# First two branches of a three-branch block: merge products that follow single y tiles, values turned behind two gate tiles, wide value products

## The reference, cut to what matters

```python
(a_q, a_f, a_i, a_z, b_q, b_k, b_v, b_o, b_ig, b_fg, b_z,
 c_r, c_k, c_v, c_wd, c_ad, c_z, g_a, g_b, g_c) = split_cols(xn @ w_in[l])
# first branch: chunked linear attention over 8 heads of 128, values a_i
y_a = head_rmsnorm(o, norm_g) * jax.nn.silu(z.astype(f32))
# second branch: 4 heads, queries and keys 128 wide, values b_v 256 wide
num = scores @ v                  # the kernel takes the whole sequence as one chunk
h = num / jnp.maximum(jnp.abs(den), jnp.exp(-m_t))[..., None]
y_b = head_layernorm(h, norm_g, NORM_EPS) * jax.nn.sigmoid(o_raw) * jax.nn.silu(z)
merged = (jax.nn.sigmoid(g_a) * (y_a @ w_br[l, 0])
          + jax.nn.sigmoid(g_b) * (y_b @ w_br[l, 1])
          + jax.nn.sigmoid(g_c) * (y_c @ w_br[l, 2]))
h = h + merged @ w_out[l]
```

## Time and profile before

| | |
|---|---|
| median of 3 runs | 3596.31 us (3595.64 to 3598.92) |
| profiled execution | 3597.59 us, span 3595.8 us |
| TensorE busy | 3515.2 us, 98% |
| TensorE weight loads | 2942.6 us, 82% |
| VectorE busy | 1504.8 us, 42% |
| ScalarE busy | 486.2 us, 14% |
| mean granted TensorE clock | 0.994 |
| line 411 (merge products) | 169.9 us busy, 9.6 us idle before |
| line 380 (gate products) | 343.5 us busy, 0.7 us idle before |

### The profile page before, as it was taken

The page is one execution under the profiler, slowest core; times in us unless marked ns, Lnnn a source line. Parts: engine busy times, 40 slices in busy tenths (PEclk is TensorE's granted clock), DMA queues, the critical chain, the costliest instruction groups (busy, mean ns, idle before and its releaser), DMA issues.

```text
span 3595.8 us, 47831 instructions
## 1 busy us (share of the span) xinstructions
PE 3515.2 (98%) x20239; PEld 2942.6 (82%) x20239; DVE 1504.8 (42%) x2787; ACT 486.2 (14%) x1113; POOL 26.9 (1%) x58
## 2 busy tenths in 40 slices
PE   7999999999999999999999999999999999999999
PEld 6888888888888998888888877777778888878877
DVE  1426531333466452513336636425233366363343
ACT  1012200011011101011001012112120010121111
POOL 1000000000000000000000000000000000000000
PEclk9999999999999999999999999999999999999999
DMA  6443244443444203644435433333444454332431
GB/s 204 140 142 117 94 141 140 145 131 106 134 136 141 72 4 127 223 133 133 148 109 160 140 117 94 92 119 106 152 139 144 120 165 140 117 117 83 135 123 71
DMA packets 436064, 454.45 MB, mean 126 GB/s; under 512 B 25227, under 2 KB 412736, under 8 KB 435328
## 3 DMA queue, kind: packets, MB, share of 16 engines
q1 hardware_dynamic: 433408, 444.68, 39.1%
q0 software_dynamic: 2144, 5.32, 0.4%
q10 hardware_dynamic: 320, 1.70, 0.1%
HBM read 449.58 MB, written 2.10 MB: 126 GB/s over the span
## 4 chain that ended last, share of the span: by engine, by line
PE 95%; DVE 2%; ACT 1%; DVEq 1%; issue 0%; ACTq 0%; DMA 0%; POOL 0%; POOLq 0%
PE bank L1798 31%; PE bank L284 18%; PE bank L380 9%; PE bank L1930 9%; PE bank L411 5%; PE bank L313 3%; PE bank L1996 3%; PE bank L1485 3%; PE bank L1045 3%; PE bank L297 2%; PE bank L1902 1%; PE bank L1983 1%; PE bank L1855 1%; PE bank L1883 1%; PE bank L1956 0%; PE bank L779 0%
## 5 line engine op out<-in xcount | busy, mean ns | idle before, releaser
L1798 PE MATMUL bank<-xnT,ring 128*128 128x272 f32 (+2 forms) x4992 | 1133.6, 389 | 0.0
L1798 PEld LDWEIGHTS bank<-xnT,ring 128*128 128x128 f32 (+1 forms) x4992 | 941.4, 189 | 188.5 <-issue 11.7
L284 PE MATMUL bank<-xnT,ring 128*128 128x272 f32 (+1 forms) x2816 | 633.2, 388 | 1.6 <-ACT wk L799 1.0
L284 PEld LDWEIGHTS bank<-xnT,ring 128*128 128x128 f32 x2816 | 534.7, 190 | 99.7 <-issue 3.3
L380 PE MATMUL bank<-xnT,ring 128*128 128x256 f32 x1536 | 343.5, 383 | 0.7 <-ACT wk L1219 0.7
L380 PEld LDWEIGHTS bank<-xnT,ring 128*128 128x128 f32 x1536 | 290.8, 191 | 41.3 <-ACT wk L1219 1.1
L1930 PE MATMUL bank<-G,ring 128*128 128x272 f32 (+1 forms) x1024 | 238.7, 388 | 0.0
L1930 PEld LDWEIGHTS bank<-G,ring 128*128 128x128 f32 x1024 | 192.8, 190 | 36.9 <-issue 3.6
L411 PE MATMUL bank<-G,ring 128*128 128x256 f32 x768 | 169.9, 385 | 9.6 <-DVEq L941 4.8
L411 PEld LDWEIGHTS bank<-G,ring 128*128 128x128 f32 x768 | 148.2, 193 | 31.1 <-DVEq L941 5.2
L460 DVE RECIPROCAL G<-G 128x272 f32<-128x272 f32 (+3 forms) x25 | 149.4, 5977 | 2.0 <-issue 0.3
(11 more groups left out here) (532 smaller groups left out, 2910.0 us busy)
## 6 DMA issues: line engine op xcount, KB each, us to landing
ring<-in_w_in SPq DMA_DIRECT2D x156, 2048.0 KB, 8.2
ring<-in_w_out SPq DMA_DIRECT2D x32, 2048.0 KB, 8.4
ring<-in_w_br SPq DMA_DIRECT2D x12, 2048.0 KB, 8.5
ring<-in_w_out SPq DMA_DIRECT2D x16, 1024.0 KB, 10.7
G<-in_x POOLq DMA_DIRECT2D x2, 1024.0 KB, 9.0
wk<-in_pool_w POOLq DMA_DIRECT2D x2, 1024.0 KB, 9.0
ring<-in_w_in SPq DMA_DIRECT2D x4, 512.0 KB, 5.7
out<-G SPq DMA_DIRECT2D x8, 256.0 KB, 2.4
```

The source lines that it names most:

```text
L284: mm = pe.matmul(bank[j][:, first:T], ring[:, s, k, j * P:(j + 1) * P], rhs[:, k, first:T], start=(k == 0), stop=(k == KT - 1))
L1798: mm = pe.matmul(out_, ring[:, s, k, c:c + m], xnT[:, k, first:T], start=(k == 0), stop=(k == KT - 1))
```

## The change

Four edits in the first two branches. The values are turned behind two of the gate tiles, no longer ahead of all, on TensorE and on ScalarE. The second branch's value products run by key tile: for key tile `i` one matmul over all queries from its start on (272, 144 and 16 columns), so 3 per output tile. The last product on y is made per tile (first branch) or per pair of tiles (second), each raising the new semaphore `y_tile`; `merge_pe` waits inside its first output tile for each of the eight tiles in turn, where it waited for `y_ready` (which stays for the third branch and for a DMA on SyncE). For that, the other factors are applied earlier: in the first branch the product with `g[6]`, and in the second the product of both gates and the norm's weight is formed in `g[6]` while sums are made; the first branch's last Exp is cut in two parts (2 and 6 tiles). Two table preloads are written out ahead of ScalarE's waits. The diff, without the line of names:

```diff
--- before.py
+++ after.py
...
@@ -401,13 +401,16 @@
                 last_use[s] = (br_full, KT * b + 4 * (s + 1))
 
         def merge_pe(pe, b, y):
-            pe.wait_ge(S["y_ready"], b + 1)
+            if b == 2:
+                pe.wait_ge(S["y_ready"], 3)
             pe.wait_ge(turn_free, turns["pe"].n + 2)
             for s in range(SLOTS):
                 pe.wait_ge(w_loaded[s], 16 * uses["pe"][s].go())
                 for j in range(4):
                     pe.wait_ge(br_free, KT * b + 4 * s + j + 1)
                     for k in range(W8):
+                        if b < 2 and s == j == 0:
+                            pe.wait_ge(S["y_tile"], W8 * b + k + 1)
                         mm = pe.matmul(bank[6 + j % 2][:, META:T], wide[:, s, k, j * P:(j + 1) * P], y[:, k, META:T],
                                        start=(k == 0), stop=(k == W8 - 1))
                     mm.then_inc(br_full, 1)
@@ -498,6 +501,7 @@
             act.drain()
             act.activation(real(g[6]), real(g[3]), ACT.Exp, scale=-1.0).then_inc(S["hg_exp"], 1)
 
+            gates_act(act, 2)
             act.wait_ge(S["stack_zero"], 3)
             for i, (t0, n) in enumerate(TT):
                 for half in range(2):
@@ -507,7 +511,7 @@
                        .then_inc(turn_free, 1)
             act.drain()
             act.nop().then_inc(S["tok_ready"], 1)
-            gates_act(act, 5)
+            gates_act(act, 3)
             for n, m in enumerate(ENDS + [None]):
                 act.wait_ge(S["hg_in"], n + 2)
                 act.wait_ge(work_full, work["act"].go(8))
@@ -528,10 +532,12 @@
             act.activation(real(g[5]), real(g[4]), ACT.Square).then_inc(S["hg_exp"], 1)
             gates_act(act, KT - 5 - len(ENDS) - 2)
             work["act"].go(8)
+            act.preload_act_table(ACT.Ln)
             act.wait_ge(S["hg_in"], len(ENDS) + 3)
             act.activation(real(g[2]), real(g[2]), ACT.Ln)
             act.drain()
-            act.activation(real(g[2]), real(g[2]), ACT.Exp, scale=-0.5).then_inc(S["hg_exp"], 1)
+            for part in (slice(0, 2), slice(2, W8)):
+                act.activation(real(g[2])[:, part], real(g[2])[:, part], ACT.Exp, scale=-0.5).then_inc(S["hg_exp"], 1)
             gates_act(act, 1)
 
         def level_blocks(m):
@@ -545,7 +551,9 @@
             return [(slice(r, r + 32), slice(r, r + 32), slice(r, r + 32)) for r in range(0, P, 32)]
 
         def hgrn_pe(pe):
-            pe.wait_ge(proj_free, tiles["pe"].n + 2)
+            evicted = tiles["pe"].n + 2
+            gates_pe(pe, 2)
+            pe.wait_ge(proj_free, evicted)
             for i, (t0, n) in enumerate(TT):
                 for half in range(2):
                     u = turns["pe"].go()
@@ -553,7 +561,7 @@
                     for j in range(4):
                         mm = pe.transpose(tbank(u)[0:n, j * P:(j + 1) * P], g[2][:, 4 * half + j, t0:t0 + n], eye)
                     mm.then_inc(turn_full, 1)
-            gates_pe(pe, 5)
+            gates_pe(pe, 3)
             pe.wait_ge(turn_free, turns["pe"].n + 2)
             for n, m in enumerate([0] + ENDS + [None]):
                 pe.wait_ge(S["hg_m"], n + 1)
@@ -688,10 +696,12 @@
             y = real(g[4])
             v.tensor_tensor(y, y, across(vec("hgrn_norm_g"), width=SEQ), ALU.mult)
             v.drain()
-            v.wait_ge(E, 6 + len(ENDS) + 2)
-            v.tensor_tensor(y, y, real(g[2]), ALU.mult)
-            v.drain()
             v.tensor_tensor(y, y, real(g[6]), ALU.mult)
+            v.drain()
+            for h in range(8):
+                if h in (0, 2):
+                    v.wait_ge(E, 6 + len(ENDS) + 2 + h // 2)
+                v.tensor_tensor(y[:, h], y[:, h], real(g[2])[:, h], ALU.mult).then_inc(S["y_tile"], 1)
             v.drain()
             v.nop().then_inc(S["y_ready"], 1)
 
@@ -740,10 +750,12 @@
 
         def mlstm_pe(pe):
             c = ml["pe"]
-            pe.wait_ge(proj_free, tiles["pe"].n + 2)
+            evicted = tiles["pe"].n + 2
+            gates_pe(pe, 2)
+            pe.wait_ge(proj_free, evicted)
             pe.wait_ge(br_free, 4 * NM + 2)
             to_tokens_pe(pe, g[1])
-            gates_pe(pe, 3)
+            gates_pe(pe, 1)
             pe.wait_ge(S["ml_pe"], c["pe"].go(2))
             u = work["pe"].go()
             pe.wait_ge(work_free, u)
@@ -770,14 +782,10 @@
                 for out_tile in range(3):
                     u = work["pe"].go()
                     pe.wait_ge(work_free, u)
-                    for q, (q0, qn) in enumerate(TT):
-                        for i in range(q + 1):
-                            n = TT[i][1]
-                            v0 = h * 256 + out_tile * P
-                            lhsT = ones[0:n, :] if out_tile == 2 else tok3[0:n, i, v0:v0 + P]
-                            at = E_AT[i][0] + q0 - E_AT[i][1]
-                            mm = pe.matmul(wbank(u)[:, q0:q0 + qn], lhsT, sc[0:n, at:at + qn],
-                                           start=(i == 0), stop=(i == q))
+                    for i, (t0, n) in enumerate(TT):
+                        v0, at = h * 256 + out_tile * P, E_AT[i][0]
+                        lhsT = ones[0:n, :] if out_tile == 2 else tok3[0:n, i, v0:v0 + P]
+                        mm = pe.matmul(wbank(u)[:, t0:T], lhsT, sc[0:n, at:at + T - t0], start=(i == 0), stop=(i == 2))
                     mm.then_inc(work_full, 1)
                 gates_pe(pe, 1)
             gate_products(pe, 8)
@@ -803,8 +811,9 @@
             act.drain()
             act.activation(ROWS[:, TMP, :], ROWS[:, TMP, :], ACT.Ln, bias=1.0).then_inc(S["ml_act"], 1)
             act.activation(real(g[6]), real(g[3]), ACT.Exp, scale=-1.0).then_inc(S["ml_act"], 1)
+            gates_act(act, 2)
             to_tokens_act(act)
-            gates_act(act, 6)
+            gates_act(act, 4)
             for h in range(B_HEADS):
                 act.wait_ge(S["ml_in"], c["in"].go())
                 sc = mlsc[h % 2]
@@ -921,6 +931,11 @@
                                        -1.0 / 256, g[4][:, 2 * h:2 * h + 2, :], ALU.mult, ALU.add).then_inc(work_free, 1)
             v.drain()
             v.nop().then_inc(S["ml_in"], 1)
+            gate = real(g[6])
+            v.tensor_tensor(gate, gate, real(g[2]), ALU.mult)
+            v.drain()
+            v.tensor_tensor(gate, gate, across(vec("mlstm_norm_g"), width=SEQ), ALU.mult)
+            v.drain()
             for h in range(B_HEADS):
                 u = work["dve"].go()
                 v.wait_ge(work_full, u)
@@ -929,15 +944,12 @@
             v.nop().then_inc(S["ml_in"], 1)
             n = 3 + B_HEADS + 1
             y = real(g[4])
-            v.tensor_tensor(y, y, across(vec("mlstm_norm_g"), width=SEQ), ALU.mult)
+            v.tensor_tensor(y, y, gate, ALU.mult)
             v.drain()
             v.wait_ge(S["ml_act"], n + 1)
-            y4 = g[4].rearrange("p (h a) t -> p h a t", a=2)[:, :, :, META:T]
-            v.tensor_tensor(y4, y4, g[0][:, 0:4, META:T].unsqueeze(2).to_broadcast([P, 4, 2, SEQ]), ALU.mult)
-            v.drain()
-            v.tensor_tensor(y, y, real(g[2]), ALU.mult)
-            v.drain()
-            v.tensor_tensor(y, y, real(g[6]), ALU.mult)
+            for h in range(B_HEADS):
+                y2 = y[:, 2 * h:2 * h + 2]
+                v.tensor_tensor(y2, y2, g[0][:, h:h + 1, META:T].to_broadcast([P, 2, SEQ]), ALU.mult).then_inc(S["y_tile"], 2)
             v.drain()
             v.nop().then_inc(S["y_ready"], 1)
 
```

4 lines of the change are left out of this document (2 added, 2 removed).

## The result

| | before | after |
|---|---|---|
| median, first comparison | 3597.61 us (3595.64 to 3604.39, 4 runs) | 3571.98 us (3571.66 to 3572.93, 4 runs) |
| profiled execution | 3597.59 us, span 3595.8 | 3571.93 us, span 3570.1 |
| TensorE busy | 3515.2 us | 3506.9 us |
| mean granted clock | 0.994 | 0.997 |

The ratio is 0.9929 (95% interval 0.9913 to 0.9944): faster beyond its interval, by 25.6 us (0.7%) where 32.3 were forecast, and at the far end of the forecast's range. Of the five gains in the forecast's sum four came in to about 0.1 us, the one of the wide products brought half, and a stretch that the change doesn't touch lost 4.7 us.

What follows compares the result with a forecast made beforehand. TensorE, busy 98% of the span, was taken to bound the kernel. Gains 4.6 + 6.7 + 7.6 + 7.2 + 6.5 less 0.3 for waits made 32.3 us: 3565.3 against the profiled execution, 3564.0 against the median, range 3559 to 3572.

Steps and rivals of the forecast that it cites:

- Turned values: Value transposes moved behind two gate tiles, hiding ScalarE's Exp: gain 4.6 us in the first branch, 6.7 in the second.
- The rival of a clock that falls behind them: TensorE's clock falls behind the moved value transposes, costing 4 us in all, so 3568; chance 0.15.
- the twin at 2117: Second block's value transposes right behind a wait: they kept clock 1.00, cited against a fall behind the moved transposes.
- Merges: Merge products follow single y tiles, removing TensorE's stop and slow first tile: gain 7.2 us first branch, 6.5 second.
- a stop that stays: TensorE still stops at both merges because a y tile is late; with half the gain kept, 3571; chance 0.06.
- two merges at the lower clock: Waits hold TensorE so loosely that both merges run at 1.2 GHz, 110 us more, 3674; chance of slower 0.02.
- Wide products: Second branch's value products, three matmuls per output tile in place of six: gain 1.90 us per head, 7.6 in all.
- For the new form a twin exists: Line 1875's three matmuls of 272, 144 and 16 columns take 0.94 us, taken as the price of a wide output tile.
- The stage's bounds of 7.1 to 10.1: Limits on the wide value products' gain in us: 7.1 by per-matmul prices, 10.1 by columns alone.
- 0.26 us per matmul whatever its width: Price read from the old value products of line 779: narrow matmuls are paid by their weight load.
- Everything behind the second merge should only be shifted: After the second branch's merge, later work keeps its lengths; a growing difference would refute that nothing later catches the gain.
- the milder rivals: Clock fall behind the transposes (3568), stop left at the merges (3571), wide products for nothing (3572); upper range end 3572.

Runs made afterwards that it cites:

- full rows: Changed kernel with the last key tile's value-product weights zero-padded from 16 to 128 rows; 3570.49 and 3569.70 us in two sittings, ratio 0.9918 both times.
- The repeats: Unedited kernels run and profiled again: the kernel before 3600.32 us, the changed kernel 3569.52 and 3569.98 us.
- merges alone: Kernel before with only the merge products following single y tiles, factors applied earlier, Exp in parts and preloads; 3590.17 us, ratio 0.9976.
- spread gate products: Changed kernel with 128-row zero-padded weights and gate products moved between narrow products of first and third branch; 3563.07 and 3565.68 us, ratios 0.9906 and 0.9899.

## Why the forecast was right, and where it was wrong

**Turned values: right, size and mechanism.** 4.54 and 6.70 us against 4.6 and 6.7. The Exp hides under two gate tiles, and the copies behind the moved gate reads delayed nobody: the third gate read waits only for TensorE. The rival of a clock that falls behind them didn't come: 1.00 in both branches in the changed kernel and with this part alone. The Trainium skill's rule ("TensorE: Matmul & The Clock Gate", part 4) that transposes don't count as busy would have had it fall each time. No trace here shows that behind the moved transposes: none of the 18 sets in the nine profiles that have them is followed by a fall. But the twin at 2117 fell in 5 of 13 profiles, so my one row against the rule was weaker evidence than I made it.

**Merges: right.** 7.04 and 6.46 against 7.2 and 6.5, less 0.15 each for the waits. No tile came late, the two preloads stand where the loads stood, and VectorE's later start of its merge loop cost TensorE nothing, though it made the read of the first tile late. The rivals of a stop that stays and of two merges at the lower clock are both refuted by the distances.

**Wide products: the term of the sum was mis-sized.** 7.6 us forecast, 3.8 measured. The failed step is "For the new form a twin exists": I matched the twin by its moving columns (272, 144, 16) and not by the shape of its weights (128 rows by 16 columns in the third, against 16 rows by 128). A tile of the change costs 1.26 us, the same tile with full rows 0.96; the other 0.30 a tile is the 16-row product, 0.88 a head and 3.5 in all. The stage's bounds of 7.1 to 10.1 were both too high for the same reason: both priced the narrow product as any other. The price was to be had in the kernel before, where the same line had mixed 16-row and 128-row weights at 0.26 a product, but only as a mean; "0.26 us per matmul whatever its width" reads more out of these rows than they show.

**Everything behind only shifted: wrong for this execution.** "Everything behind the second merge should only be shifted" failed by 4.7 us in the third branch, and the first branch had 3.1 to the good by the same kind of event. The step behind it is the use of one profiled execution's clock as the kernel's own. I counted the lowered clock behind each stop as gone (2.42 and 1.7 us at the merges, in the 7.2 and 6.5), which holds at the place, and took all other falls as fixed. Behind the removed stops the first held in every profile. The repeats show that the others are not fixed: the kernel before is at 0.50 near 404 in one profile and at 1.00 in another, and its time spreads from 3593 to 3609 us. With merges alone both distances give 13.5 us, and the kernel 9.9 by the means.

**The account.** Against the profiled execution the forecast was 3565.3 and the result 3571.93, 6.6 us apart: 3.8 the wide products, 4.7 the third branch, 0.7 the later start, 0.5 behind the third branch, less 3.1 near 404. Against the median it is 8.0, since the profiled execution of before lay 1.28 above the median of three runs. That base was itself low: 46 runs of the kernel before have a mean of 3600.0. The forecast's range was made from the milder rivals and a spread of 3.3 us seen in three runs; the spread in 46 runs is 16 us, and the range had no room for a mis-sized term and a poor draw of the clock together.

**What stays open.** What decides, from one execution to the next, whether a weak stretch (narrow products, transposes) falls and for how long; why the merges alone gave back some 4 us of clock elsewhere; and why full rows, which removed 3.5 us of work, raised the loss to the clock by 5.0 us over nine runs. The first sitting of the experiments ran on another chip than the two later ones, and for the first comparison the record names none, so some of the differences between profiles could be the chip's. Not all can: the two profiles with spread gate products come from one chip, and one has falls near 404 and 1278 that the other has not.

## What to carry to other kernels

Price a matmul by a row with the same shape of weights as well as the same moving columns. Where a contraction ends in a short tile between full ones, try padding it with zeros to 128 rows: here it shortened the stage by 0.88 us a head, though the kernel's time didn't show it. Write down which part of an expected gain is work and which is clock: the work arrives to a tenth of a microsecond, the clock only on average, and a single profile doesn't tell which falls stand in every execution. Here those behind the removed stops and on the 16-row products did, those on other narrow products and on transposes came and went. Work that must be done anyway, set between such products, took 6.0 us off the mean here.

## What the runs showed that I had not expected

- A product with 16 rows of weights and 16 columns between 128-row ones costs 0.30 us more than the same product with 128 rows: 1.26 against 0.96 us a tile of three, 3.77 against 2.89 a head.
- TensorE's clock can fall to 1.2 GHz while it is busy: 3.00 of 3.00 us at 0.50 (1293 to 1302 after the change, 1.4 us behind a stop of 0.84), on products with 16-row weights, and at 1286 on 64x64 tiles with no stop just ahead.
- Two executions of one kernel differ in which stretches fall, at 404 and 2117 in both directions, with hardly any difference in the sum (0.994 both times), while the falls behind the four removed stops stood in every profile that has these stops.
- Less work does not have to mean less time where TensorE bounds the kernel at 98%: full rows, net 5.5 us shorter by the estimate, time 0.6 us shorter (standard error 0.9).
